# Prompt scores over 128 contracted rows: rounded keys stacked on their low parts, queries from a DRAM buffer

## The reference, cut to what matters

```python
s = jnp.einsum('bqgjd,bcgd->bgjqc', q5, kc)              # compressed keys
s = jnp.einsum('bqgjd,bgqnkd->bgjqnk', q5, kg)           # selected blocks (keys k_sel)
s = jnp.einsum('bqgjd,bkgd->bgjqk', q5, kw)              # window (keys k_win)
p = masked_softmax(s, mw[None, None, None])
o_win = jnp.einsum('bgjqk,bkgd->bqgjd', p.astype(vw.dtype), vw)
o = g[..., 0:1] * o_cmp + g[..., 1:2] * o_sel + g[..., 2:3] * o_win
```

## Time and profile before

| | |
|---|---|
| median of 3 runs | 544.44 us (543.87 to 544.52) |
| the profiled execution's own time | 547.66 us |
| its span, first to last instruction | 545.9 us |
| TensorE busy | 526.0 us (96%), granted clock 0.993 on the mean |
| VectorE busy | 331.4 us (61%) |
| ScalarE busy | 241.7 us (44%) |
| GpSimd busy | 156.9 us (29%) |
| DMA | 81.05 MB moved, 148 GB/s on the mean |

### The profile page before, as it was taken

How to read it: one execution, slowest core, us unless ns; L and a number is a source line. 1 busy time by engine, 2 the same in 40 slices (tenths; PEclk the granted TensorE clock), 3 DMA queues, 4 the chain that set the end, 5 groups by cost and what they waited for, 6 DMA issues and landing times.

```text
span 545.9 us, 12830 instructions
## 1 busy us (share of the span) xinstructions
PE 526.0 (96%) x5198; PEld 475.2 (87%) x5198; DVE 331.4 (61%) x840; ACT 241.7 (44%) x561; POOL 156.9 (29%) x257
## 2 busy tenths in 40 slices
PE   6899999999999999989989999999999999999995
PEld 4899999999899999887987876767788999999995
DVE  4543222479698784685474588587863477763466
ACT  6534424534531422241232778677774432223334
POOL 0005843033513544545000065664364000000000
PEclk9899999999999999999999999999999999999998
DMA  8526662347535373886322167563554534406104
GB/s 303 203 79 199 198 235 78 135 129 251 199 98 193 108 226 116 256 306 199 150 79 78 40 154 190 141 165 87 156 138 103 157 116 137 134 1 194 40 6 161
DMA packets 59789, 81.05 MB, mean 148 GB/s; under 512 B 7825, under 2 KB 49233, under 8 KB 59218
## 3 DMA queue, kind: packets, MB, share of 16 engines
q1 hardware_dynamic: 48320, 49.97, 29.9%
q0 software_dynamic: 10688, 29.14, 17.4%
q10 hardware_dynamic: 722, 1.12, 0.6%
HBM read 65.23 MB, written 8.13 MB: 134 GB/s over the span
## 4 chain that ended last, share of the span: by engine, by line
PE 89%; DVE 5%; DMA 2%; issue 2%; ACT 1%; POOL 0%; DVEq 0%; ACTq 0%
PE m L1723 61%; PE so L2021 4%; PE so L2030 3%; PE so L1894 2%; PE so L1897 2%; PE so L1895 2%; PE m L1807 2%; PE so L1933 2%; DMA U<-in_ck_cmp,cmp_rows 1%; PE so L1871 1%; PE so L1981 1%; PE t L1859 1%; DVE w_lo L1307 1%; PE t L1749 1%; PE so L2007 1%
## 5 line engine op out<-in xcount | busy, mean ns | idle before, releaser
L1723 PE MATMUL m<-h_hi,w_hi 128*128 128x272 f32 x448 | 132.7, 296 | 1.1 <-DVE za L1420 0.8
L1723 PE MATMUL m<-h_hi,w_lo 128*128 128x272 f32 x448 | 129.2, 288 | 0.0
L1723 PE MATMUL m<-h_lo,w_hi 128*128 128x272 f32 x448 | 128.7, 287 | 0.0
L1723 PE MATMUL m<-w_hi,h_hi 128*128 128x256 f32 (+2 forms) x360 | 105.0, 292 | 2.4 <-issue 1.9
L1723 PE MATMUL m<-w_lo,h_hi 128*128 128x256 f32 (+2 forms) x360 | 102.9, 286 | 0.0
L1723 PE MATMUL m<-w_hi,h_lo 128*128 128x256 f32 (+2 forms) x360 | 102.8, 286 | 0.0
L1307 DVE TENSOR_TENSOR w_lo<-raw,w_hi 128x1024 fp32r<-128x1024 f32 (+2 forms) x62 | 71.0, 1154 | 42.4 <-ACT w_hi L1044 38.5
L1723 PEld LDWEIGHTS m<-h_hi,w_hi 128*128 128x128 f32 x448 | 84.3, 188 | 13.5 <-issue 10.2
L1000 POOL DMA_DIRECT2D U<-p_turn x108 | 58.2, 547 | 103.5 <-DVE p_turn L1629 102.1
L1723 PEld LDWEIGHTS m<-h_lo,w_hi 128*128 128x128 f32 x448 | 84.5, 189 | 0.0
L1723 PEld LDWEIGHTS m<-h_hi,w_lo 128*128 128x128 f32 x448 | 84.5, 189 | 0.0
(11 more groups left out here) (300 smaller groups left out, 903.1 us busy)
## 6 DMA issues: line engine op xcount, KB each, us to landing
raw<-in_w_in SPq DMA_DIRECT2D x36, 512.0 KB
U<-in_x_p SPq DMA_DIRECT2D x8, 512.0 KB, 5.3
raw<-in_w_o SPq DMA_DIRECT2D x8, 512.0 KB
U<-p_turn POOLq DMA_DIRECT2D x54, 64.0 KB, 2.6
U<-p_turn SPq DMA_DIRECT2D x42, 64.0 KB, 2.8
raw<-in_w_in SPq DMA_DIRECT2D x8, 256.0 KB
raw<-in_w_pa SPq DMA_DIRECT2D x8, 256.0 KB
raw<-in_w_pb SPq DMA_DIRECT2D x4, 512.0 KB
```

Of the source, the lines that this page charges most:

```text
L1723: ins = mm(out, lhs(a, k), rhs(b, k), start=(k == 0 and a + b == 0), stop=(k == n - 1 and a == 1))
```

## The change

- The unit order in a tile becomes jh, then y, so that two units in a row share their queries.
- Keys: a new item `ks` behind the third `main` group after the queries' transposes. ScalarE waits until the queries are stored, then rounds each group's keys into `k_st` [128, 2 groups, 2 branches, 512] in rows 64g to 64g+63 (which takes the place of `qT`); VectorE subtracts, in place of `kT` (`k_lo`); GpSimd moves each group's low parts by DMA to the other 64 rows of `k_st`.
- Queries: with the item `qTs` SyncE stores `qT` in DRAM (`q_dram`, two DMAs of 512 KB). For each pair of units (one tile, one jh) an item `ql` loads the four heads' 128 queries back, once for each half of the rows (two DMAs of 128 KB); an item `qh` splits them: ScalarE rounds (`q_h`), VectorE subtracts in place (`q_l`). Two buffers take turns.
- Scores: a head's scores are two fp32r matmuls of 128 contracted rows and 128 queries, `q_h` and then `q_l` against `k_st`: rounded keys in one half of the rows and their low parts in the other, each times the same queries.
- The compressed scores read `q_plain`, the queries of one tile loaded back by an item `qc` (four DMAs of 64 KB) into the place of two tensors that are no longer read.

```diff
+    order += [("ks",), ("hid", 0), ("w1lo", 0)]
...
+    order += [("ql", 0), ("qkS", 0)]
...
                 if q == NQ - 1:
+                    order += [("qc", 0), ("cs", 0)]
...
+            order += [("s_out", q), ("qkS", 1), ("qh", 0)]
...
-    units = [(i, y, jh) for i in TILES for y in range(2) for jh in range(2)]
+    units = [(i, y, jh) for i in TILES for jh in range(2) for y in range(2)]
...
+    order += [("ql", 1), ("cx", 0)]
...
         if n == 0:
             order += [("ct", k, 0), ("ct", k, 1)]
+            if k < NT - 1:
+                order += [("qc", k + 1)]
+        if u % 2:
+            if m + 1 < len(units) // 2:
+                order += [("ql", m + 1)]
+            if m < len(units) // 2:
+                order += [("qh", m)]
         order += [("px", u)]
...
+        k_st = placed("k_st", 0, [P, G, 2, TP], F32R)
+        k_lo = placed("k_lo", 2048, [P, 2, TP], F32R)
+        q_f = [placed(f"q_f{n}", 2048 + 1024 * n, [P, J, P]) for n in range(2)]
+        q_l = [placed(f"q_l{n}", 2048 + 1024 * n, [P, J, P], F32R) for n in range(2)]
+        q_h = [placed(f"q_h{n}", 2560 + 1024 * n, [P, J, P], F32R) for n in range(2)]
...
+                elif s[0] == "qTs":
+                    for i in range(NT):
+                        wait_evacuated(sp, T_AT[("qT", i)])
+                    for g in range(G):
+                        sp.dma_start(q_dram[:, :, g, :], qT[64 * g:64 * g + 64, :, :]).then_inc(q_saved, 16)
+                elif s[0] == "ql":
+                    m = s[1]
+                    i, _, jh = UNITS[2 * m]
+                    if m == 0:
+                        sp.wait_ge(k_moved, 32)
+                    elif m == 1:
+                        sp.wait_ge(o_done, NQ)
+                    else:
+                        sp.wait_ge(p_scored, 2 * J * (m - 1))
+                    src = q_dram[:, 2 * jh:2 * jh + 2, :, tok(i)].rearrange("d j g t -> d (j g) t")
+                    for a in (slice(0, 64), slice(64, 128)):
+                        sp.dma_start(q_f[m % 2][a, :, :], src).then_inc(q_loaded[m % 2], 16)
+                elif s[0] == "qc":
+                    i = TILES[s[1]]
+                    if s[1]:
+                        sp.wait_ge(t_done, T_AT[("cs", s[1] - 1)] + 1)
+                    else:
+                        sp.wait_ge(qk_done, NQ)
+                        sp.wait_ge(main_done, MAIN_AT[rows_of(SLOT["V1"])] + 1)
+                        sp.wait_ge(q_saved, 32)
+                    for n in range(2):
+                        for g in range(G):
+                            sp.dma_start(q_plain[n][64 * g:64 * g + 64, :, :], q_dram[:, 2 * n:2 * n + 2, g, tok(i)]).then_inc(q_plain_loaded, 16)
...
+                elif s[0] == "ks":
+                    pool.wait_ge(k_lo_done, 1)
+                    for g in range(G):
+                        a, b = slice(64 * g, 64 * g + 64), slice(64 - 64 * g, 128 - 64 * g)
+                        pool.dma_start(k_st[b, g, :, :], k_lo[a, :, :]).then_inc(k_moved, 16)
...
+                elif kind == "ks":
+                    for y in range(2):
+                        wait_evacuated(act, T_AT[("kT", y)])
+                    act.wait_ge(q_saved, 32)
+                    for g in range(G):
+                        r = slice(64 * g, 64 * g + 64)
+                        ins = nc.scalar.copy(k_st[r, g, :, :], kT[r, :, :])
+                    ins.then_inc(k_hi_done, 1)
+                elif kind == "qh":
+                    m = s[1]
+                    act.wait_ge(q_loaded[m % 2], 32 * (m // 2 + 1))
+                    nc.scalar.copy(q_h[m % 2][:, :, :], q_f[m % 2][:, :, :]).then_inc(q_hi_done, 1)
...
+                elif kind == "ks":
+                    dve.wait_ge(k_hi_done, 1)
+                    for g in range(G):
+                        r = slice(64 * g, 64 * g + 64)
+                        ins = v.tensor_tensor(k_lo[r, :, :], kT[r, :, :], k_st[r, g, :, :].bitcast(F32), ALU.subtract)
+                    ins.then_inc(k_lo_done, 1)
+                elif kind == "qh":
+                    m = s[1]
+                    dve.wait_ge(q_hi_done, m + 1)
+                    v.tensor_tensor(q_l[m % 2][:, :, :], q_f[m % 2][:, :, :], q_h[m % 2][:, :, :].bitcast(F32), ALU.subtract).then_inc(q_lo_done, 1)
...
                 elif kind == "cs":
+                    pe.wait_ge(q_plain_loaded, 16 * 4 * (s[1] + 1))
...
-                    for c in range(2):
-                        for g in range(G):
-                            k = J * u + 2 * jj + g
-                            if k >= 3 and c == 0:
-                                pe.wait_ge(p_masked, k - 2)
-                            r, q = slice(64 * g, 64 * g + 64), slice(i * P + 64 * c, i * P + 64 * c + 64)
-                            ins = mm(S[k % 3][64 * c:64 * c + 64, 0:n], qT[r, 2 * jh + jj, q], kT[r, y, 0:n], start=True, stop=True)
+                        pe.wait_ge(k_moved, 32)
+                    if u % 2 == 0 and jj == 0:
+                        pe.wait_ge(q_hi_done, m + 1)
+                        pe.wait_ge(q_lo_done, m + 1)
+                    for g in range(G):
+                        k = J * u + 2 * jj + g
+                        if k >= 3:
+                            pe.wait_ge(p_masked, k - 2)
+                        for x in (q_h, q_l):
+                            ins = mm(S[k % 3][:, 0:n], x[m % 2][:, 2 * jj + g, :], k_st[:, g, y, 0:n], start=(x is q_h), stop=(x is q_l))
+                        ins.then_inc(p_scored, 1)
```

More of the change, by code:

```diff
@@ L269, in plan @@
     main(3)
-    order += [("hid", 0), ("w1lo", 0)]
+    order += [("ks",), ("hid", 0), ("w1lo", 0)]
     for c in range(1, NCH):
@@ L302, in plan @@
     main(2)
-    order += [("qkS", 0)]
+    order += [("ql", 0), ("qkS", 0)]
     for q in range(NQ):
@@ L314, in plan @@
                 if q == NQ - 1:
-                    order += [("cs", 0)]
+                    order += [("qc", 0), ("cs", 0)]
             main(1)
@@ L326, in plan @@
             main(1)
-            order += [("s_out", q), ("qkS", 1)]
+            order += [("s_out", q), ("qkS", 1), ("qh", 0)]
     for q, name in enumerate(("ZB0", "RA0")):
@@ L338, in products @@
         order.extend(("pp", u, kt) for kt in range(units[u][0] + 1))
-    order += [("cx", 0)]
+    order += [("ql", 1), ("cx", 0)]
     for u in range(len(units)):
         n, k = u % 4, u // 4
+        m = u // 2 + 1
         order += [("ps", u, 0)]
@@ L510, in nsa_gmlp_layer @@
      sk_cmp, sv_cmp, sk_sel, sv_sel, sk_win, sv_win, s_chunk) = outs
+    q_dram = nc.dram_tensor("q_dram", (DH, J, G, TP), F32, kind="Internal").ap()
     ctx = ExitStack()
@@ L558, in nsa_gmlp_layer @@
         kT = placed("kT", 2048, [P, 2, TP])
+        k_st = placed("k_st", 0, [P, G, 2, TP], F32R)
[3 more added lines that the diff above has]
+        q_h = [placed(f"q_h{n}", 2560 + 1024 * n, [P, J, P], F32R) for n in range(2)]
+        q_plain = [x[:, :, :].rearrange("p k t -> p (k t)").rearrange("p (j n) -> p j n", j=2) for x in (h_rows, q_bd)]
         v_tok = placed("v_tok", 4096, [P, 2, NT + 1, P])
@@ L666, in nsa_gmlp_layer @@
         mix_ready = sem("mix_ready")
+        q_saved, k_hi_done, k_lo_done, k_moved = sem("q_saved"), sem("k_hi_done"), sem("k_lo_done"), sem("k_moved")
+        q_loaded, q_hi_done, q_lo_done = [sem("q_loaded0"), sem("q_loaded1")], sem("q_hi_done"), sem("q_lo_done")
+        q_plain_loaded = sem("q_plain_loaded")
         m_sum, m_hi, m_lo = sem("m_sum"), sem("m_hi"), sem("m_lo")
@@ L1988, in _ @@
                     i = TILES[s[1]]
-                    if s[1] == 0:
-                        wait_evacuated(pe, T_AT[("qT", NT - 1)])
-                        wait_evacuated(pe, T_AT[("kT", 1)])
+                    pe.wait_ge(q_plain_loaded, 16 * 4 * (s[1] + 1))
                     for j in range(J):
-                        ins = mm(tb[:, j * 2 * NCP:(j + 1) * 2 * NCP].rearrange("p (g n) -> p g n", g=G), qT[:, j, tok(i)], kcp[:, :, :], start=True, stop=True)
+                        ins = mm(tb[:, j * 2 * NCP:(j + 1) * 2 * NCP].rearrange("p (g n) -> p g n", g=G), q_plain[j // 2][:, j % 2, :], kcp[:, :, :], start=True, stop=True)
                     ins.then_inc(t_done, 1)
@@ L2012, in _ @@
                     n = (i + 1) * P
+                    m = u // 2
                     if u == 0 and jj == 0:
                         pe.wait_ge(s_exp, NQ)
-                    for c in range(2):
-                        for g in range(G):
-                            k = J * u + 2 * jj + g
-                            if k >= 3 and c == 0:
-                                pe.wait_ge(p_masked, k - 2)
-                            r, q = slice(64 * g, 64 * g + 64), slice(i * P + 64 * c, i * P + 64 * c + 64)
-                            ins = mm(S[k % 3][64 * c:64 * c + 64, 0:n], qT[r, 2 * jh + jj, q], kT[r, y, 0:n], start=True, stop=True)
-                            if c:
-                                ins.then_inc(p_scored, 1)
+                        pe.wait_ge(k_moved, 32)
```

(1 more changed line is left out.)

## The result

The changed kernel takes 571.12 us (median of 5 runs, 569.11 to 575.14) against 544.44 (5 runs, 543.87 to 545.89): ratio 1.0496, 95% interval 1.0445 to 1.0548. That is 27 us more, where the prediction said 9 more and a range of 545 to 560. (A few executions in this document's sets, the kernel before's among them, take over 700 us; they are left out of every time and ratio.) The profiled execution, the slowest of the five, spans 573.4 us against 545.9.

A forecast was written before the change was run, and what follows sets the result against it. TensorE, busy nearly all the span, with 89% of the last chain its own queue, bounds the kernel. Attention +6.0 (12.1 - 4.5 - 1.6), first load +1.5, keys' split +1.5: +9.0 us, 544.44 to 553.4, range 545 to 560.

The forecast's parts named there:

- (1): Prompt attention's score blocks: the new form saves TensorE 4.5 us, and 1.6 us of old mask waits go.
- that rival: Narrow score blocks: 128-column matmuls run like fp32, 0.25 us each, 4 us more, 557.4; chance 0.13.
- the lower price that the prediction set beside its own for 512 columns: Eight wide score blocks: by the skill's 131 ns per matmul, 0.52 us instead of 0.90, saving 3 us more.
- (2): Ahead of even units: TensorE waits for the query splits at seven places, 12.1 us, none at unit 6.
- (3): Compressed scores: TensorE waits 3.4 us for the first q_plain load, +1.5 us net; three later loads hidden.
- (4): Keys' split ahead of the compressed branch's first weights: their low part starts 2.1 us late, +1.5 us.
- (5): Query store, GpSimd's copies, first split, SyncE's extra DMAs: cost nothing; a store landing after 110.2 adds to (4).
- the late-store rival: Keys' split: ScalarE waits for the queries' store, landing at 112 instead of 110.2, 1.8 us more, 555.2; chance 0.04.
- The three rivals on the slow side: Narrow blocks like fp32, 557.4, chance 0.13; TensorE loses its clock, 559, 0.10; queries stored late, 555.2, 0.04.
- clock rival: Waits over 3 us at unit 2 and compressed scores: TensorE at half clock, 6 us more, 559; chance 0.10.

The follow-up runs named there:

- e12: e8 with each later load of the split's queries ahead of its unit's seven block moves on SyncE's queue: 539.42 us against 542.65 before, ratio 0.9938.
- e2: Changed kernel with each q_plain load issued as early as its buffer is free: 562.14 us, ratio 1.0294 to the kernel before.
- e4: Changed kernel with 127 useless matmuls added ahead of waits at units 2, 4, 12, 14 and the first and last compressed scores: 566.08 us, ratio 1.0376.
- e7: Kernel before with only the queries' store to DRAM and the q_plain loads for the compressed scores: 558.52 us, ratio 1.0261.
- e5: Changed kernel with the three edits of e1, e2 and e3 together: 545.25 us, ratio 1.0011 to the kernel before.
- e8: e5 with ScalarE's rounding of the queries one unit earlier, ahead of the even unit's exponentials: 546.96 us, ratio 1.0086 to the kernel before.
- e11: e5 with each later load of the split's queries ahead of its unit's seven block moves on SyncE's queue: 540.61 us, ratio 0.9971.
- e1: Changed kernel with each query split right behind the odd unit's first score block instead of behind the transposes: 564.69 us, ratio 1.0348.
- e3: Changed kernel with the keys' split 90 us later in the order, behind the first six key blocks: 566.71 us, ratio 1.0404.

## Why the prediction was wrong

**(1), the score form and the old mask waits: right in sum.** Without waits (e12's timeline against that of before) the attention's main groups take 3.3 us less, the score blocks 0.2, transposes and compressed scores 0.5: 4.0 in all, forecast 4.5. Its two halves were off against each other. The blocks save 0.2 instead of 1.9, because the forecast took 0.90, 0.69 and 0.48 us for all of them, and only a block with full-array work on both sides goes like that (0.93, 0.70, 0.47). One beside a value product or right behind a compressed step takes 1.02 to 1.04 at 512 columns, 0.78 to 0.82 at 384 and 0.56 to 0.58 at 256. The borders gone save 3.8 instead of 2.6. The Trainium skill's "TensorEngine Tiling (Array Packing)", section Key Properties, says that a change of tiling mode drains TensorE; the borders that went agree. It is not all of it, since a block behind the compressed scores, which use the full array too, also takes 0.09 more; what that is stays open. The narrow blocks took 0.49 us; that rival is false, and so is the lower price that the prediction set beside its own for 512 columns, since the wide blocks took 0.93 and not 0.52. Of the kernel before's mask waits (1.9 us, counted as lost time) none is left in the changed kernel, as forecast; but that was so because TensorE stood at the splits instead. In e12, which has no such waits, they are back with 2.7, and 0.4 for a block move.

**(2), the waits for the splits: right in place, and their sum too, but the clock behind them was missing. This is the largest failed step.** 3.62, 2.22, 1.06, 1.82 and 2.31 us at units 2, 4, 8, 12 and 14, none at 6 and 10: 11.0 us against 12.1. (At unit 10 the wait for q_plain just ahead hides it; in e2, without that wait, it is 0.34.) What failed is that the price of a wait was taken as its length. The six waits of 1.8 us and more, the loads' among them, are 18.2 us long and cost 9.8 more in the groups behind them, and 12.7 with the blocks and compressed scores. The prediction put this at nothing in its sum and had it as a rival with a tenth of the chance, with "one group at each of two places" for 6 us. It came at all six, at 0.9 to 2.5 us a group instead of 3. e4 shows the cause. The argument for a low chance was that no row of these stages showed it, which is no argument, since before the change no wait there cost more than 0.9 us.

**(3), the compressed scores' loads: the second failed step.** The first load's +1.5 became 5.0: the wait was 4.1 (forecast 3.4), the scores and the group behind it ran 2.7 longer at the lower clock, and the old waits and shorter steps behind them gave back 1.7 (forecast 1.9). SyncE's four issues came as forecast: they ended at 280.1, 0.8 us after TensorE's arrival (forecast 0.9). The loads took longer, 3.9 to 4.1 us from issue to landing instead of the 3.1 that the forecast's times allow. Worse, "the three later loads stand four blocks ahead of their use and are hidden" was false for two of them, 0.42 and 4.09 us, with 1.0 of clock in the group behind the last. Standing early in the order is not being issued early. The rows to see it were there: the load stands behind a unit's seven moves, those wait for its transposes, and in the timeline of before the transposes in question end at 371.3; with 4.5 for the moves, 2.6 for four issues and 2.8 to land that is 381.2, where TensorE arrives at 376.6: 4.6 us. e7 shows (3) by itself, clock included: 14 us.

**(4) and (5), the keys' split: mis-sized by 2.5 us.** 4.0 against 1.5. The store of a megabyte took until 111.0, 8.2 us from its issue at 102.8, and the ScalarE copies, forecast for ScalarE's idle time ahead of 112.47, began at 111.07 and ended at 113.2; on the times of the kernel before that is 112.5 and 114.6, 2.2 late. So the late-store rival was true as well, at about its forecast price of 1.8; it had a chance of 0.04.

**The sum.** The keys cost 4.0 and the first load 5.0. The attention's 19.6 are 15.5 us of waits, less 4.0 saved by the form and 1.9 of old mask waits, and the rest, 10.0, is what ran slower behind the waits: 7.6 in the groups, the remainder in score blocks, compressed scores and the last matmuls ahead of the waits. Together 28.6, less the 1.4 that this execution was ahead at the start: 27.2 of 27.5. The forecast had 9.0. Of the 18.5 between them 12.7 are the clock, 5.2 the waits for q_plain (4.5 of them at the two places called hidden) and 2.5 the keys; the splits' waits took 1.1 less, the start gave 1.4, and small terms are left (0.6). The three rivals on the slow side were priced as alternatives to the forecast, and two of them came true beside it. That the time of 559 in the clock rival's line is nearest to the measured one says little, since its places and its price per place were both off.

## What to carry to other kernels

When TensorE sets the end, price a new wait as its length plus the slow stretch that may follow it (here 18.2 us of waits and 12.7 behind them), and count both at every place, not at the longest alone. For each new DMA, ask what stands ahead of it on the issuing queue and what that waits for: here the cure was five moves in an order (the three of e5, the rounding of e8, the split's loads of e11), and the same kernel went from 5% slower to 0.6% faster without a change to its arithmetic. And a wait that is taken away can come back at the next late load, as in e1, so look at the whole chain of waits before pricing the cure of one. Rivals that act on the same engine add up, so give the range their sum.

## What the runs showed of the hardware

The length of a wait does not decide alone whether the clock falls. In these stages it stayed behind the waits of 1.06 us at unit 8, and fell behind each of over 3 us (3.62 to 5.12). Between them it varies: it fell behind 1.31 us in e5 and behind 1.46 in e1 but not behind 1.46 in e5; it stayed behind 2.96 us in e1 and 2.52 in e8; behind 2.31 us at unit 14 it fell in the changed kernel and in e2 (groups of 4.60 and 4.46) and stayed in e3 (3.09); and behind 2.2 us at unit 4 it fell in the changed kernel and stayed in e2, with the same work ahead. TensorE at that wait in both, first the changed kernel, then e2:

```profile
343.48 0.41 PE L2096 MATMUL so<-k_st,q_h 128*128 128x384 f32 x1 [2.22 <-issue]
...
344.50 0.42 PE L1796 MATMUL m<-h_hi,w_lo 128*128 128x272 f32 x1
344.72 0.43 PE L1796 MATMUL m<-h_hi,w_hi 128*128 128x272 f32 x1
```

```profile
341.35 0.41 PE L2096 MATMUL so<-k_st,q_h 128*128 128x384 f32 x1 [2.23 <-issue]
...
342.37 0.29 PE L1796 MATMUL m<-h_hi,w_lo 128*128 128x272 f32 x1
342.50 0.29 PE L1796 MATMUL m<-h_hi,w_hi 128*128 128x272 f32 x1
```

The fall also comes with a delay: here a microsecond after work had begun again, at unit 2 before it had. This would fit with the spread of the runs, 6 us for the changed kernel and 2 us for the one before, which no run tests; what decides it stays open.
